# A hybrid decoder layer on one core: instruction order around the selection, paired memory scores, quarter-size merge tiles

## The chip, the core and the metric

The kernel runs on one core of a Trainium2 chip. Its engines work side by side, each through its own list of instructions in the order in which the program issued them: TensorE (PE, with its weight loads PEld), VectorE (DVE), ScalarE (ACT), GpSimd (POOL) and SyncE (SP), which starts the DMA transfers. They meet only at semaphores. The metric is the time of one execution in microseconds (us); lower is better.

## The reference, cut to what matters

```
h = x @ w_in                                  # 1024 x 1024 tokens, 14 column groups
# A: gated DeltaNet, 4 heads x 128, chunked delta rule
g    = -exp(a_log) * softplus(a + dt_bias);   g = cumsum(g) per chunk
m    = I + strict_lower(k_beta @ k^T * decay) # solved against v*beta and k_beta*exp(g)
S    = S * exp(g_last) + k_dec^T @ (u - w @ S)    # scan over the chunks
# B: sparse attention, 4 heads x 64 over a shared latent of rank 128
score = sum_j relu(q_idx_j . k_idx) * w_j     # indexer, 8 heads x 64, causal
idx   = top_k(score, 256)                     # which keys a query may see
o_s   = softmax(q_abs . c[idx] / 8 - slope * dist) @ c[idx], then @ w_uv
# C: cross attention, 4 heads x 64, into 256 memory tokens
o_m   = softmax(q_m @ k_m^T / 8) @ v_m
y = concat(rmsnorm(o_a) * silu, o_s * silu, o_m * silu) @ w_out
x = layernorm(alpha * x + y)
```

Instead of gathering, the kernel finds for every query the value of its 256th largest score and turns the scores into masks.

## The kernel before

The 1024 tokens are 8 blocks of 128. `make_plan` (L127) writes one list of steps such as `("proj", h, part, t, s)`; each engine walks the list and issues what it has to do for a step. So the order of a step in the list is its order in every engine's queue, and the list is all that sets the order. The stages, with their time in the profile:

- 0 to 80 us: loads, splitting of x and weights into a high and a low half (`split` on ScalarE, `low` on VectorE; three matmuls, L1025 to L1027, make one product), the projections for the indexer.
- 80 to 152 us: the index scores (`idx`): 2 matmuls into a bank (L1017), a ReLU on ScalarE (L1851), a weighted sum on VectorE (L1466). Between them stand projections of head 0, the memory keys and values (`kmT`, `vm`) and the gates (`gate_sums`: two matmuls, four small operations on VectorE L1546 to L1550, three exponentials on ScalarE L1881 to L1883; `knorm`).
- 152 to 575 us: for each of the 4 DeltaNet heads the inverse of a triangular matrix is merged in levels 4, 5 and 6. `M` multiplies (L1188), ScalarE copies the product out, `XY` multiplies with the copy (L1201, L1203), VectorE subtracts (L1630, L1632). Then comes a scan over 8 blocks (`scanV`, `scanS`). A scan step goes from PE to VectorE and back twice. The function `woven` (L228) puts projections of the next head (`proj`, `side`) between these steps as fill.
- In the same stretch the selection runs: 32 rounds, one for each bit of a float. A round counts, on ScalarE, the scores above a candidate for 6 blocks (L1863, in three groups of two blocks: `count`), then VectorE makes the next candidate (`update`, L1472 to L1489; in the last round a chain of dependent operations up to L1506). ScalarE of a round waits for VectorE's update, and the update waits for all six counts. `woven` puts a group of counts into a fill whenever `owed`, raised by `SELECT_RATE` per fill, reaches 1.
- After round 31: `reach` (one pass over the scores of a block, L1512), `threshold`, and six passes for each of 6 blocks (`dm`, L1668 to L1683), all on VectorE, woven into head 3.
- 575 to 821 us: attention by blocks in the order 3, 4, 2, 5, 1, 6, 0, 7: scores `sc`, memory scores `msc` (L1270; in two halves by head parity, 64 rows of contraction each), transposes, the latent sum `lat`, the output `o`, and the output projection `y` (L1340 to L1342) with layer norm. `merged` interleaves the queues of one block's attention, the next block's scores and the block before's projection. The weights of `y` are split in 8 pieces (`split out0` to `out7`: 128x1024 on ScalarE, then on GpSimd L2115).

PSUM has 8 banks, dealt out in turn by pools (`pools`): "D": 4 to 7 for `idx`, `At`, `M`, `XY`, `nw`, the scan and two of the three `tok` transposes; "A": 4, 5, 6 for `msc`, `mixT`, `pT`, `mpT`. A matmul into a bank waits until the use before it has been read.

## Time and profile before

| | us |
|---|---|
| median of 3 runs (817.15 to 823.08) | 821.11 |
| profiled execution, its own time | 822.64 |
| its span, first to last instruction | 820.8 |
| PE busy | 757.1 |
| VectorE busy | 493.4 |
| ScalarE busy | 454.9 |

The span is 1.84 us shorter than the time of the same execution. PE is the busiest engine by far, so the time is PE's own work, plus the time in which PE waits, plus what PE loses where its granted clock is 1.2 GHz instead of 2.4 GHz (0.50 in the column PEclk).

### The profile page before, as it was taken

The numbers are of one execution on the slowest core, as the hardware profiler recorded it, in microseconds if no ns is written. First come the engines' busy times: TensorE is split into PE (matmuls) and PEld (weight loads), VectorE is DVE, ScalarE is ACT, GpSimd is POOL, SyncE is SP. The second block draws the span as 40 slices with busy tenths as digits, with TensorE's granted clock in tenths as the row PEclk, the third lists the DMA queues.
The fourth block names the chain that finished last, engine by engine and source line by source line (L and its number), as shares of the span: only waits on it lengthen the run. The fifth ranks groups of instructions, "written<-read, shape, count | busy, mean of one in ns | idle before, by whom it ended". The sixth has DMA issues, their size and how long they took to land.

```text
span 820.8 us, 11387 instructions
## 1 busy us (share of the span) xinstructions
PE 757.1 (92%) x3940; PEld 623.1 (76%) x3940; DVE 493.4 (60%) x1076; ACT 454.9 (55%) x1027; POOL 178.6 (22%) x272
## 2 busy tenths in 40 slices
PE   6999999899899999988999898987789999989993
PEld 5888888688798788877798687865567777767772
DVE  5633889775557484564646449594744644754533
ACT  4532776787768975988568971222752332433310
POOL 0000000162003610251103520000376134312320
PEclk9999999999899999999899996999989999999997
DMA  9312111034002330024000351010951322231110
GB/s 362 117 52 78 51 39 65 0 98 119 26 27 68 85 116 26 27 81 135 26 27 27 93 161 40 26 46 25 334 161 40 110 71 86 77 94 52 65 51 26
DMA packets 63913, 65.86 MB, mean 80 GB/s; under 512 B 16368, under 2 KB 49392, under 8 KB 63472
## 3 DMA queue, kind: packets, MB, share of 16 engines
q1 hardware_dynamic: 63856, 65.13, 24.7%
q8 instruction: 32, 0.52, 0.3%
q14 instruction: 25, 0.20, 0.1%
HBM read 48.35 MB, written 16.78 MB: 79 GB/s over the span
## 4 chain that ended last, share of the span: by engine, by line
PE 60%; DVE 17%; ACT 11%; issue 10%; DMA 1%; POOL 0%; SPq 0%; ACTq 0%; DVEq 0%; POOLq 0%
PE bank L1025 8%; PE bank L1026 8%; PE bank L1027 8%; PE bank L1017 6%; ACT cst L1863 5%; PE bank L1340 4%; PE bank L1031 4%; PE bank L1341 4%; PE bank L1342 4%; PE bank L1290 3%; PE bank L1203 3%; DVE score L1466 2%; PE bank L1201 2%; PE bank L1188 2%; ACT ring_split L1780 1%
## 5 line engine op out<-in xcount | busy, mean ns | idle before, releaser
L1025 PE MATMUL bank<-x_hi,ring_split 128*128 128x512 f32 x480 | 201.4, 420 | 8.5 <-DVE x_lo L1415 7.3
L1026 PE MATMUL bank<-x_lo,ring_split 128*128 128x512 f32 x480 | 191.7, 399 | 0.0
L1027 PE MATMUL bank<-x_hi,ring_split 128*128 128x512 f32 x480 | 191.7, 399 | 0.0
L1863 ACT ACTIVATE cst<-score,sel 128x896 bf16<-128x896 f32 (+3 forms) x192 | 167.1, 874 | 34.2 <-DVE sel L1488 32.6
L1025 PEld LDWEIGHTS bank<-x_hi,ring_split 128*128 128x128 f32 x480 | 93.4, 195 | 25.2 <-DVE ring_split L1419 7.3
L1027 PEld LDWEIGHTS bank<-x_hi,ring_split 128*128 128x128 f32 x480 | 92.8, 193 | 20.7
L1026 PEld LDWEIGHTS bank<-x_lo,ring_split 128*128 128x128 f32 x480 | 93.5, 195 | 15.8
L1780 ACT ACTIVATE arena<-bank 128x512 f32<-128x512 f32 x77 | 44.0, 590 | 72.7 <-PE bank L1031 50.3
L2046 POOL TENSOR_TENSOR arena<-arena,hsc 128x512 f32<-128x512 f32 x8 | 8.3, 1038 | 269.7 <-ACT arena L1933 269.7
L1340 PE MATMUL bank<-w_out_hi,mix_hi 128*128 128x512 f32 x128 | 58.5, 457 | 5.4 <-DVE mix_lo L1729 5.4
L2033 POOL TENSOR_TENSOR arena<-arena,cst 128x512 f32<-128x512 f32 x24 | 32.6, 1377 | 103.2 <-PE bank L1188 53.3
L1466 DVE SCALAR_TENSOR_TENSOR score<-arena,wis,score 128x384 f32<-128x384 f32 (+3 forms) x70 | 46.0, 657 | 9.6 <-ACT arena L1851 3.2
L1341 PE MATMUL bank<-w_out_lo,mix_hi 128*128 128x512 f32 x128 | 51.2, 400 | 0.0
L1342 PE MATMUL bank<-w_out_hi,mix_lo 128*128 128x512 f32 x128 | 51.0, 398 | 0.0
L1031 PEld LDWEIGHTS bank<-cst,arena 128*128 128x128 f32 x320 | 38.7, 145 | 12.4 <-issue 6.8
L1031 PE MATMUL bank<-cst,arena 128*128 128x128 f32 x320 | 47.0, 281 | 1.0 <-ACT arena L1980 0.6
L1419 DVE TENSOR_TENSOR ring_split<-ring,ring_split 128x1024 fp32r<-128x1024 f32 x30 | 37.9, 1264 | 7.5 <-ACT ring_split L1780 7.1
L1851 ACT ACTIVATE arena<-bank 128x384 f32<-128x384 f32 (+3 forms) x80 | 36.6, 529 | 8.8 <-PE bank L1017 6.7
L1971 ACT ACTIVATE arena<-arena,misc 128x512 f32<-128x512 f32 (+7 forms) x32 | 24.8, 774 | 26.7 <-DVE misc L1698 26.6
L1472 DVE TENSOR_TENSOR sel<-sel 128x6 f32<-128x6 f32 x32 | 11.8, 368 | 42.3 <-ACT cst L1863 42.3
L1290 PE MATMUL bank<-arena,small 128*128 128x512 f32 x72 | 36.8, 602 | 0.3 <-DVE arena L1706 0.3
L1863 ACT ACTIVATION_READ_ACCUMULATOR cst<-score,sel 128x1 f32 x192 | 36.7, 191 | 0.0
(274 smaller groups left out, 1477.9 us busy)
## 6 DMA issues: line engine op xcount, KB each, us to landing
ring<-in_w_groups SPq DMA_DIRECT2D x30, 512.0 KB, 3.5
x_raw<-in_x_t SPq DMA_DIRECT2D x8, 512.0 KB, 8.8
side_z<-stage SPq DMA_DIRECT2D x16, 256.0 KB, 2.1
w_out_sb<-in_wout_t SPq DMA_DIRECT2D x2, 2048.0 KB, 11.1
zgT<-side_z SPq DMA_DIRECT2D x8, 512.0 KB, 3.9
qkvT<-in_x SPq DMA_DIRECT2D x8, 512.0 KB, 3.3
out_y<-arena SPq DMA_DIRECT2D x8, 512.0 KB, 2.9
ring<-in_wmem_t SPq DMA_DIRECT2D x2, 1024.0 KB, 4.6
```

The source lines that it names most:

```text
L1017: last = nc.tensor.matmul(dst, w, r, start=(i == 0), stop=(i == len(pairs) - 1))
L1025: nc.tensor.matmul(dst, hi, xh, start=(c == 0), stop=False)
L1026: nc.tensor.matmul(dst, hi, xl, start=False, stop=False)
L1027: last = nc.tensor.matmul(dst, lo, xh, start=False, stop=(c == KT - 1))
L1031: return nc.tensor.transpose(dst, src, ident[0:n, 0:n])
L1290: last = nc.tensor.matmul(ps(key)[:, :], sm[:, kt, 0:P], pTb[(order[e] - 1) % 3], start=(kt == 0), stop=(kt == b))
L1340: nc.tensor.matmul(ps(key)[:, :], mh, wout_hi[:, c, half], start=(c == 0), stop=False)
L1341: nc.tensor.matmul(ps(key)[:, :], mh, wout_lo[:, c, half], start=False, stop=False)
L1342: last = nc.tensor.matmul(ps(key)[:, :], ml, wout_hi[:, c, half], start=False, stop=(c == KT - 1))
L1466: last = v.scalar_tensor_tensor(score[:, at + lo:at + hi], r[:, 0:hi - lo], w, score[:, at + lo:at + hi], ALU.mult, ALU.add)
L1780: return sc.activation(dst, src, ACT.Copy, scale=scale)
L1863: sc.activation(signs[order[e] % 2][:, 0:w], score[:, score_at(b):score_at(b + 1)], ACT.Sign, scale=-1.0, bias=candidate[:, b - 2:b - 1], ...
```

## The change

- `gate_sums` stands some units earlier in the index stage; its three exponentials are a step of their own, `gate_exps`, that follows all index tiles.
- `SELECT_RATE` is 0.90 (0.88). In the fill before `M` of level 4 no counts are put; they come behind it (a fill of length 0).
- `reach` and `dm` are single steps, put in by a budget (`MASK_KEYS` keys per unit of fill) instead of pairs per fill.
- The last merge level multiplies 64x64 quarters: `M` and `XY` of level 6 use 64 rows and 64 columns of each block, and the copy is 64x256 (128x512).
- `msc` of both halves of a block is one step that alternates the two row halves; it waits for both banks first, and at block 3 only for the memory keys; the values are waited for at `o`.
- The splits of the output weights: two while block 3's attention runs (four), six in the next block.

```diff
-SELECT_RATE = 0.88
+SELECT_RATE = 0.90
+MASK_KEYS = 1350
@@ make_plan
-    selection += [[("reach", 7), ("reach", 2)], [("reach", 6), ("reach", 3)], [("reach", 5), ("reach", 4), ("threshold",)]]
-    selection += [[("dm", b, i), ("dm", b, i + 1)] for b in SELECT_ORDER for i in (0, 2, 4)]
+    selection += [[("reach", b)] for b in range(NB - 1, 2, -1)] + [[("reach", 2), ("threshold",)]]
+    selection += [[("dm", b, i)] for b in SELECT_ORDER for i in range(6)]
...
-    first_work = [*keys, [("kmT",)], [("gates",)], *queries, [("vm",)], [("silu", 0, 0)], [("gate_sums",)], [("knorm", 0)]]
+    first_work = [*keys, [("kmT",)], [("gates",)], *queries, [("gate_sums",)], [("vm",)], [("silu", 0, 0)], []]
...
+    add(("gate_exps",))
+    add(("knorm", 0))
...
+    def mask_cost(e):
+        return (e[1] + 1) * P * (2 if e[0] == "dm" and e[2] == 2 else 1)
+
+    def masks(keys):
+        owed[1] = min(owed[1] + keys, 2 * SEQ)
+        while selection and not due and owed[1] >= mask_cost(selection[0][0]):
+            owed[1] -= mask_cost(selection[0][0])
+            select()
...
-            if silus[0] == 0 and s[2]:
+            if selection and selection[0][0][0] != "count":
+                if s[2]:
+                    masks(int(MASK_KEYS * s[1]))
+            elif silus[0] == 0 and s[2]:
                 owed[0] -= select(int(owed[0] >= 1))
...
-        steps = [*pair("At", h), *pair("tok", h, 0), ("diag_load", h), 1, 1, *pair("tok", h, 2), 1, 1]
+        steps = [*pair("At", h), *pair("tok", h, 0), ("diag_load", h)]
+        steps += [1, 1, *pair("tok", h, 2), 1] if more else [("fill", 1, None)] * 2 + [*pair("tok", h, 2), ("fill", 1, None)]
+        steps += [("fill", 1, 0)]
...
-            steps += [*pair("M", h, s), 1.5, QUIET if s == NLEV - 1 and more else 1.5]
+            steps += [*pair("M", h, s), *([("fill", 0, SELECT_RATE)] if s == LEV0 else []), 1.5, QUIET if s == NLEV - 1 and more else 1.5]
...
-            at[place:place] = [[("msc", nb, 0)], [("msc", nb, 1)]]
+            at[place:place] = [[("msc", nb, 0), ("msc", nb, 1)]]
...
-            out = [[("split", f"out{i}")] for i in range(4)]
+            out = [[("split", f"out{i}")] for i in range(2)]
...
-                for i in range(4):
-                    out[i].append(("split", f"out{i + 4}"))
+                for i, at_unit in enumerate((0, 0, 1, 2, 4, 5)):
+                    out[at_unit].append(("split", f"out{i + 2}"))
@@ TensorE, M and XY of the last level
+                            last = nc.tensor.matmul(ps(e)[0:64, i * 64:(i + 1) * 64], uo[0:64, 64:P], x_[0:64, 0:64], start=True, stop=True)
...
+                            m1 = row(a, R_M1)[64:P, i * 64:(i + 1) * 64]
+                            last = nc.tensor.matmul(ps(e)[0:64, i * 64:(i + 1) * 64], m1, blk(row(a, R_Y), i)[64:P, 64:P], start=True, stop=True)
@@ TensorE, msc
-                            pe.wait_ge(side_mem_back, 32)
+                        pe.wait_ge(mem_keys_back, 16)
...
+                    for m in range(2):
+                        for i, half in enumerate(halves):
+                            rows_ = slice(64 * i, 64 * i + 64)
+                            last = nc.tensor.matmul(ps(half)[:, m * 256:(m + 1) * 256], q_mem(PLACE[b])[rows_, m, :],
+                                                    kmT[rows_, m * 256:(m + 1) * 256], start=True, stop=True)
@@ ScalarE
+                    if s == NLEV - 1:
+                        copy(row(a, R_M1)[64:P, 0:256], ps(e)[0:64, 0:256]).then_inc(release_of(e), 1)
```

How it moves instructions, at three places. First ScalarE's queue in head 0, before level 4: the L1863 rows are counts (two per group), the `arena<-bank 128x512 x2` row is the copy of the two `M` tiles. Before:

```order
L1780 ACTIVATE hbuf<-bank 128x512
L1863 ACTIVATE cst,sel<-score,sel 128x1024
L1863 ACTIVATE cst,sel<-score,sel 128x384
L1863 ACTIVATE cst,sel<-score,sel 128x896
L1863 ACTIVATE cst,sel<-score,sel 128x512
L1780 ACTIVATE arena<-bank 128x512 x2
L1863 ACTIVATE cst,sel<-score,sel 128x768
L1863 ACTIVATE cst,sel<-score,sel 128x640
```

And in the change (its lines are 37 further down):

```order
L1817 ACTIVATE hbuf<-bank 128x512
L1900 ACTIVATE cst,sel<-score,sel 128x1024
L1900 ACTIVATE cst,sel<-score,sel 128x384
L1817 ACTIVATE arena<-bank 128x512 x2
L1900 ACTIVATE cst,sel<-score,sel 128x896
L1900 ACTIVATE cst,sel<-score,sel 128x512
```

One group of counts stands behind the copies instead of ahead of them. The second place is VectorE's queue at the start of head 3. The row `arena<-bank,arena 128x512 x2` is the evacuation of the two `At` tiles; the rows on `sel` are the update of round 31. Before:

```order
L1399 TENSOR_TENSOR o_head<-o_head,bank 128x128 x2
L1373 TENSOR_TENSOR arena<-bank,arena 128x512 x2
L1472 TENSOR_TENSOR sel<-sel 128x6
L1483 TENSOR_TENSOR sel<-sel 128x6
L1484 TENSOR_SCALAR sel<-sel 128x6
```

And in the change, from the long custom operation of that update on:

```order
L1535 ISA sel<-sel 128x12
L1536 TENSOR_TENSOR sel<-sel 128x6
L1537 TENSOR_TENSOR sel<-sel 128x6
L1538 TENSOR_TENSOR sel<-sel 128x6
L1539 TENSOR_TENSOR sel<-sel 128x6
L1540 TENSOR_TENSOR sel<-sel 128x6
L1546 TENSOR_SCALAR qkvT,sel<-score,sel 128x1024
L1407 TENSOR_TENSOR arena<-bank,arena 128x512 x2
```

The whole update and the first `reach` now stand ahead of the two evacuations. The third place is PE's queue at the first memory scores (block 3), with the banks. Before:

```order
L1270 MATMUL bank4<-kmT_64,arena 128x256 x2
L1017 MATMUL bank2<-key_stack,q_hi_odd_blocks_67 128x320
L1017 MATMUL bank2<-key_stack,q_odd_blocks_lo_59 128x320
L1017 MATMUL bank3<-key_stack,q_hi_odd_blocks_67 128x320
L1017 MATMUL bank3<-key_stack,q_odd_blocks_lo_59 128x320
L1270 MATMUL bank5<-kmT_64,arena 128x256 x2
```

And in the change:

```order
L1302 MATMUL bank4<-kmT_64,arena 128x256
L1302 MATMUL bank5<-kmT_64,arena 128x256
L1302 MATMUL bank4<-kmT_64,arena 128x256
L1302 MATMUL bank5<-kmT_64,arena 128x256
L1039 MATMUL bank2<-key_stack,q_hi_odd_blocks_67 128x320
```

The two halves stand together and alternate between banks and row halves.

## Rows read from the trace of the kernel before

**Rows 1.** The page, part 1: busy us, share of the span, instructions.
```profile
PE 757.1 (92%) x3940; PEld 623.1 (76%) x3940; DVE 493.4 (60%) x1076; ACT 454.9 (55%) x1027; POOL 178.6 (22%) x272
```
**Rows 2.** Timeline of PE: start, us, what, [idle before <- releaser]; its waits.
```profile
148.63 0.79 PE L1017 MATMUL bank<-khi,q 128*128 128x512 f32 x1 [2.71 <-ACT arena L1851]
...
208.82 0.43 PE L1201 MATMUL bank<-arena 128*128 128x64 f32 x2 [2.47 <-ACT arena L1780]
...
398.71 0.43 PE L1201 MATMUL bank<-arena 128*128 128x64 f32 x2 [1.63 <-ACT arena L1780]
...
496.33 0.41 PE L1201 MATMUL bank<-arena 128*128 128x64 f32 x2 [1.91 <-DVE arena L1612]
...
544.52 0.80 PE L1238 MATMUL bank<-vnew,arena 128*128 128x128 f32 x2 [2.27 <-DVE vnew L1637]
...
558.25 0.79 PE L1238 MATMUL bank<-vnew,arena 128*128 128x128 f32 x2 [2.86 <-DVE vnew L1637]
...
582.17 1.13 PE L1270 MATMUL bank<-kmT,arena 64*128 64x256 f32 x4 [1.21 <-DMA vm<-side_mem]
...
601.43 1.08 PE L1309 MATMUL bank<-wuv,arena 128*128 128x64 f32 x8 [3.17 <-ACT arena L1780]
```
**Rows 3.** Stretches: span, busy us of PE, PEld, DVE, ACT, POOL, PEclk, DMA.
```profile
148.60:151.60 3.00, 2.97 (x8) 2.29 (x9) 2.68 (x4) 2.82 (x8) 0.00 (x0) 0.50 0.00 0
209.70:216.60 6.90, 6.90 (x31) 6.51 (x31) 5.31 (x15) 6.28 (x15) 0.00 (x0) 0.51 0.00 0
...
401.30:407.60 6.30, 6.30 (x22) 5.43 (x22) 5.87 (x15) 3.78 (x7) 0.00 (x0) 0.50 0.00 0
```
**Rows 4.** Timeline of VectorE: the last index sums.
```profile
148.61 5.88 DVE L1466 SCALAR_TENSOR_TENSOR score<-arena,wis,score 128x512 f32<-128x512 f32 x7 [1.02 <-ACT arena L1851]
```
**Rows 5.** Timeline of ScalarE: counts and the copies of M, heads 0 and 2.
```profile
206.46 1.03 ACT L1863 ACTIVATE cst<-score,sel 128x896 bf16<-128x896 f32 x1
...
208.19 1.06 ACT L1780 ACTIVATE arena<-bank 128x512 f32<-128x512 f32 x2
...
396.33 1.15 ACT L1863 ACTIVATE cst<-score,sel 128x1024 bf16<-128x1024 f32 x1 [4.14 <-DVE sel L1488]
```
**Rows 6.** Stretches around head 3, and the scan of head 2.
```profile
478.70:486.90 8.20, 7.81 (x49) 6.64 (x48) 1.77 (x5) 8.15 (x19) 0.00 (x0) 1.00 0.65 168
...
487.90:562.10 74.20, 66.01 (x329) 55.14 (x327) 63.07 (x112) 16.25 (x31) 4.42 (x4) 0.86 0.13 44
...
454.00:473.00 19.00, 14.76 (x84) 12.25 (x83) 10.18 (x34) 17.92 (x45) 8.90 (x31) 1.00 0.30 81
```
**Rows 7.** Timeline of VectorE: evacuation of At, update of round 31, reach, the masks' hole.
```profile
480.94 1.28 DVE L1373 TENSOR_TENSOR arena<-bank,arena 128x512 f32<-128x512 f32 x2
486.88 0.17 DVE L1472 TENSOR_TENSOR sel<-sel 128x6 f32<-128x6 f32 x1 [4.66 <-ACT cst L1863]
...
492.33 1.28 DVE L1512 TENSOR_SCALAR_CACHE_REDUCE qkvT<-score,sel 128x1024 f32<-128x1024 f32 x1
...
532.02 1.39 DVE L1560 SCALAR_TENSOR_TENSOR key_stack<-bank,key_stack 64x512 fp32r<-64x512 f32 x2 [4.64 <-ACT key_stack L1780]
```
**Rows 8.** Timeline of ScalarE: the last weight split ahead of block 3's output.
```profile
599.75 1.05 ACT L1780 ACTIVATE w_out_hi<-w_out_sb 128x1024 fp32r<-128x1024 f32 x1
```
**Rows 9.** Timeline of PE: M and XY of level 6 (head 0), one half of msc.
```profile
232.93 1.95 PE L1188 MATMUL bank<-arena 128*128 128x128 f32 x16
...
238.82 1.90 PE L1203 MATMUL bank<-arena 128*128 128x64 f32 x16
...
650.36 1.13 PE L1270 MATMUL bank<-kmT,qmT 64*128 64x256 f32 x4
651.41 0.33 PE L1031 MATMUL bank<-cst,arena 128*128 128x128 f32 x1
```
**Rows 10.** Waits over the whole span: who for whom, us in total, times, longest.
```profile
DVE sel L1472 <- ACT cst L1863: 42.3, 22, 4.7
...
ACT cst L1863 <- DVE sel L1488: 32.6, 22, 4.1
```

More of the change, by code:

```diff
@@ L237, in woven @@
             at += s[1]
-            owed[0] += s[2]
-            update()
+            owed[0] += s[2] or 0
+            if s[2] is not None:
+                update()
             while todo and n_units - len(todo) < n_units * at / whole:
@@ L1187, in _ @@
                     for i in range(4):
-                        last = nc.tensor.matmul(ps(e)[:, i * P:(i + 1) * P], blk(row(a, R_UO[s % 2]), i), blk(row(a, R_X), i), start=True, stop=True)
+                        uo, x_ = blk(row(a, R_UO[s % 2]), i), blk(row(a, R_X), i)
+                        if s < NLEV - 1:
+                            last = nc.tensor.matmul(ps(e)[:, i * P:(i + 1) * P], uo, x_, start=True, stop=True)
+                        else:
+                            last = nc.tensor.matmul(ps(e)[0:64, i * 64:(i + 1) * 64], uo[0:64, 64:P], x_[0:64, 0:64], start=True, stop=True)
                     last.then_inc(fill_of(e), 1)
@@ L1941, in _ @@
                     act.wait_ge(*filled(e))
[L1942 removed]
+                    if s == NLEV - 1:
+                        copy(row(a, R_M1)[64:P, 0:256], ps(e)[0:64, 0:256]).then_inc(release_of(e), 1)
+                    else:
+                        copy(row(a, R_M1), ps(e)[:, :]).then_inc(release_of(e), 1)
                 elif k == "nw":
```

53 lines of the change are left out of this document (28 added, 25 removed).

## The prediction, made before the changed kernel ran

> **What bounds the kernel now.** I read the page's first part first: PE is busy 757.1 of 820.8 us, VectorE 493.4, ScalarE 454.9 [rows 1]. PE is idle 63.9 in all, and that is where an edit of order can gain. Then PE's timeline with its waits: the long ones stand at four kinds of place, behind the last index tile, at the first multiply of a merge level (L1201), in head 3's scan (L1238) and at the entry to block 3's attention [rows 2]. Then the granted clock by stretches: behind such waits PE runs at 1.2 GHz for some us, for instance 6.9 us long behind the wait of 2.47 [rows 2, 3]. PE is busy there without a break and does half as much, so a stretch of 6.9 costs 3.4 beside the wait itself. Last, VectorE's and ScalarE's timelines at these places, for what the wait ends on [rows 4, 5, 7, 8]. The selection has its own pair of waits, VectorE for ScalarE 42.3 us and ScalarE for VectorE 32.6 [rows 10]; PE works through nearly all of them.
>
> **Part by part.** The sum goes against the profiled execution: span 820.8, own time 822.64. The median is 821.11, 1.5 less, and gains are taken off the median for the predicted time.
>
> *1. Gate exponentials behind the index tiles.* ScalarE held the ReLU for gate work that waited for VectorE; PE waited 2.71 for it and ran at half clock from 148.6 to 151.6, 1.5 lost [rows 2, 3]. Both together, 4.2, are the most that it can give. But VectorE is late itself there: its only idle in the last index sums is the 1.02 ahead of seven sums of 5.88 [rows 4], and what PE needs next is built on VectorE behind them. So the wait moves to head 0's first product instead of going. I take the 1.02 that VectorE can win: **-1.0**; ends 0 and -4.2.
>
> *2. One group of counts less ahead of the copies of M.* In head 0 PE waits 2.47 for the copies, which stand behind counts of about 1 us each; in head 2 1.63 [rows 2, 5]. Two counts behind the copies instead of ahead of them is 2 x 1.03: the first wait falls to about 0.6 (-1.8; a few tenths of the copies' 1.06 stay on the path), the second goes (-1.6). The half clock behind them costs 6.9/2 = 3.4 and 6.3/2 = 3.1 [rows 3]. Together -9.9. The counts don't vanish: they land later, in scans where ScalarE is busy 17.92 of 19.0 us [rows 6] and PE already has 4.2 idle. A quarter comes back there: **-7.4**; ends 0 and -9.9.
>
> *3. Head 3 and the masks.* From 487.9 to 562.1 PE is busy 66.0 of 74.2 at a mean clock of 0.86 [rows 6]; 0.14 x 74.2 = 10.4 of it is lost to the clock, so the work in it is 55.6 and 18.6 is the most that can go. Its waits for VectorE are 1.91, 2.27 and 2.86 [rows 2], each behind a pair of mask passes. VectorE is busy 63.1 of these 74.2, and only 1.77 of the 8.2 before [rows 6], so masks that start up to 6.4 earlier have room, and so has the hole of 4.64 at 532 [rows 7]. Against it stands a **new wait**: the update of round 31 (486.88 to 492.33, 5.45) and the first reach (1.28) now stand on VectorE ahead of the evacuation of At, which was done at 482.2 [rows 7]. Behind that evacuation are tok's second part on PE, which needs At's bank, and everything that follows it. PE has about 3 of the 7.81 us of work of that stretch in front of it, so it stalls about 6.7 - 3.0 = 3.7, and a half-clock stretch like the others' costs 3.4 more. That leaves 18.6 - 7.1 = 11.5. VectorE's chain (63.1 of busy time that cannot start before 481.5) ends no earlier than 544.6 even without one gap, and a scan step goes over it twice, so I take half: **-6.0**. Ends +3 (the stall of 7.1 and a gain of only 4 of the three waits' 7.0) and -12.
>
> *4. Memory values waited for later.* The wait of 1.21 for vm's transfer [rows 2] moves to block 3's output, 20 us on, where the transfer has landed: **-1.2**; end 0, if the keys are as late.
>
> *5. Fewer weight splits at the entry.* PE waits 3.17 at L1309 for a copy that stands behind a split of 1.05 [rows 2, 8]. Two of four splits are gone there. One was directly in front, so half of the wait or so goes: **-1.5**; ends 0 and -6.6, the wait and a half-clock stretch of 3.4 behind it.
>
> *6. Memory scores of both halves together.* One half costs PE 1.05 (650.36 to 651.41, where the next matmul starts) [rows 9]; 16 of them are 16.8. Each uses 64 of the 128 rows. If the two halves run side by side, 8.4 go; if PE takes them one after the other as now, nothing. No row of before shows two row halves in alternation, so these are the ends, 0 and -8.4. I take three quarters, **-6.4**: there are 8 passages with a start and a tail that only one half has, and the alternation is the arrangement in which two halves could overlap. The pair needs both banks at once: a few short waits at mixT go and one at the second bank comes, **-0.7**.
>
> On this the page "TensorEngine Tiling (Array Packing)" of the Trainium skill, section Key Properties, says that different tiles can load weights and multiply in parallel. By that rule term 6 would be the full 8.4, and the time 2 us less; no row of before shows it.
>
> *7. Quarter tiles of the last level.* M with 128 columns takes 1.95 for 16 records and XY with 64 columns 1.90 [rows 9]. Half the columns save 0.05. So columns are not what is paid for here, and fewer rows are not either as far as any row tells: **0**. Ends: if both halved, 4 heads x 3.85 / 2 = -7.7; if each change of tile shape costs about one record of 0.12, 16 changes are +1.9. The copy of M is half as wide on ScalarE and may give some tenths at L1203.
>
> The same page, section Instruction Overhead, gives each matmul a floor of about 60 cycles, and says not to take a tiling factor from a dimension that is already small. That speaks against this part, and the rows agree with it: 1.90 against 1.95. Key Properties adds that a change of tiling mode drains TensorE, which would be the +1.9 end.
>
> *8. Six splits in the next block.* GpSimd takes their low halves and each column half of y is multiplied as its split lands. If every one is in time, that costs nothing (the cover is block 4's attention), as four of them already do now. **0**; a late one costs a wait of about 1, the time of a split [rows 8].
>
> Sum: -1.0 - 7.4 - 6.0 - 1.2 - 1.5 - 6.4 - 0.7 = **-24.2**; 821.1 - 24.2 = 796.9, so **797**.
>
> **Rivals.**
>
> *A. The start of head 3 eats term 3* (0.16). The update and the reach hold At's banks longer than I think, because the counts of round 31 end no earlier than now: evacuation at 492.3 + 1.3, ten us late. The gain of 6.0 goes: 803. For it: [rows 7] shows VectorE waiting 4.66 for the last counts. Against: the rate of the selection is raised a little.
>
> *B. Row halves don't run side by side* (0.12). 6.4 come back: 803.3. For it: the 64-row halves now cost as much for each record as any other shape, so nothing shows that PE gives a free half away.
>
> *C. They overlap fully and short waits go too* (0.06): 2.0 less, 795. This is the skill's rule above.
>
> *D. The waits only move* (0.10). The M copies' 7.4 return in ScalarE's full scans, and head 3 and the exponentials give nothing, -1.2 - 1.5 - 6.4 - 0.7 = -9.8, and half of the overlap is gone too, -6.6: 814.5, within 1%. With the whole overlap it would be 811, just outside it.
>
> *E. Slower: the selection's rounds* (0.06). Each round is a closed loop, counts on ScalarE, update on VectorE [rows 10]. With copies ahead of counts, a round's last count comes later by up to the copies' 1.06 [rows 5]; if every one of 31 rounds grows by 1.1 us and the end of the selection pushes the masks and so head 3, that is +34 against -24: 831, 10 slower. It decides from 24.2/31 = 0.8 us a round. Against it: a fill before level 4 comes four times, not 31, and the 42.3 us of waiting in the loop can take up most of that.
>
> The forecast itself has 0.50, with a range of its own of 787 to 806.
>
> **Numbers.** The predicted time is the forecast's, 797. The unknown ends are 8.4 and 7.7 below for terms 6 and 7, 4 to 6 for terms 1, 3 and 5; they don't fall together, so the low end is 12 below: **785**. Upward, A and B together are 809, and part of D belongs to the range: **812**. Left out are E, the upper half of D, and the two tails: about 0.2. One per cent, about what a measurement of this kernel can tell from no change, is 8.2 us. Faster by more than that (below 812.9): forecast, A, B and C, 0.84. Within: D, 0.10. Slower: E, 0.06.
>
> **What would show it.** Term 1: the wait of 2.71 at L1017 is gone, and a similar one stands at head 0's first product. Term 2: the waits at L1201 of heads 0 and 2 under 1 us, and no stretch at 0.50 behind them. Term 3: a new PE wait of 3 to 4 us some us after 480, released by VectorE's evacuation of At (L1407); the waits of vnew below 1 us; the stage from 478.7 to 562.1 six us shorter. Term 4: no wait on vm. Term 5: L1309's counterpart under 2 us. Term 6: msc's two halves together take about 1.2 instead of 2.1. Term 7: 16 records of 64x64 at 1.9 to 2.0. I'm wrong if the new wait at head 3's start is over 8 us, if the pair of halves takes 2.1, or if quarter records cost about half, which would put the time near 789.

## The result, and the profile after

| | median, us | runs | against before (95% interval) |
|---|---|---|---|
| before | 820.67 | 817.15 to 823.08 | |
| changed | 793.17 | 790.73 to 794.88 | 0.9666 (0.9622 to 0.971) |

The change saves 27.5 us, or 3.3%. The prediction was 797 with a range of 785 to 812. The profiled execution took 792.68 us, its span is 790.9 (before: 820.8), so 29.9 us are to be explained.

The first part of the page of the changed kernel, against [rows 1]:

```profile
PE 729.5 (92%) x3940; PEld 597.4 (76%) x3940; DVE 484.8 (61%) x1076; ACT 454.6 (57%) x1027; POOL 181.7 (23%) x272
```

PE is busy 27.6 us less with as many instructions; its idle time fell by 2.3 only, from 63.7 to 61.4. So nearly all of the gain is PE working faster: at 2.4 GHz where it had 1.2, two row halves at once, smaller tiles. The clock is the largest part of it. The mean granted clock is 0.965 in the profile before and 0.987 in this one, which is 57 us at 1.2 GHz before and 21 after; half of the difference, 18 us, is my estimate of what the clock gave back. Most of the waits that I had counted off came back elsewhere.

The same by stage. I cut both traces where PE starts the product At of each head (L1175 before, L1197 after) and the first memory scores. Columns: span, busy us (and count) of PE, PEld, VectorE, ScalarE, GpSimd, granted clock, DMA share, GB/s. Before:

```profile
163.90:258.30 94.40, 91.19 (x503) 79.23 (x504) 58.26 (x132) 72.77 (x151) 23.07 (x43) 0.96 0.21 64
258.30:348.60 90.30, 88.53 (x532) 76.75 (x531) 55.83 (x132) 73.34 (x169) 24.12 (x43) 1.00 0.22 67
348.60:448.20 99.60, 93.46 (x532) 80.68 (x531) 56.45 (x135) 74.42 (x170) 23.68 (x43) 0.95 0.20 61
448.20:582.17 133.97, 116.56 (x613) 96.34 (x611) 89.00 (x197) 60.33 (x144) 20.63 (x43) 0.92 0.25 74
582.17:820.80 238.63, 215.68 (x1072) 163.44 (x1072) 125.50 (x293) 81.95 (x205) 81.94 (x91) 0.96 0.28 92
```

And after:

```profile
163.40:252.80 89.40, 87.22 (x503) 74.50 (x504) 57.65 (x132) 72.35 (x151) 23.55 (x43) 1.00 0.22 68
252.80:341.70 88.90, 87.27 (x532) 75.19 (x531) 55.99 (x139) 74.95 (x172) 24.30 (x43) 1.00 0.23 68
341.70:431.10 89.40, 87.11 (x532) 75.32 (x531) 53.52 (x135) 76.91 (x176) 24.49 (x43) 1.00 0.22 68
431.10:550.39 119.29, 107.89 (x614) 88.22 (x612) 84.95 (x189) 54.68 (x130) 22.19 (x43) 0.99 0.26 79
550.39:790.90 240.51, 208.84 (x1072) 158.47 (x1072) 124.45 (x293) 83.02 (x209) 81.97 (x91) 0.97 0.28 93
```

Up to the first cut 0.5 is gained; heads 0 to 3 gain 5.0, 1.4, 10.2 and 14.7. The last stage, attention, is **1.9 longer**, though its memory scores became 8.4 cheaper. That is the surprise of this result: 10 us were given back in a stage that the prediction had at -8.6 in all.

Where attention gave it back shows in PE's lines with the idle time before them (columns: count, busy us, mean ns, idle before and its releasers). Before, the output `o` and the output projection `y`:

```profile
L1309 PE MATMUL bank<-wuv,arena 128*128 128x64 f32 x64 | 8.1, 269 | 3.2 <-ACT arena L1780 3.2
L1340 PE MATMUL bank<-w_out_hi,mix_hi 128*128 128x512 f32 x128 | 58.5, 457 | 5.4 <-DVE mix_lo L1729 5.4
```

After:

```profile
L1342 PE MATMUL bank<-wuv,arena 128*128 128x64 f32 x64 | 9.0, 288 | 6.2 <-ACT arena L1817 6.2
L1374 PE MATMUL bank<-w_out_hi,mix_hi 128*128 128x512 f32 x128 | 57.3, 448 | 10.2 <-DVE mix_lo L1766 7.7 <-POOL w_out_lo L2155 1.9 <-issue 0.6
```

The idle time ahead of `o` grew by 3.0, ahead of `y` by 4.8.

PE's timeline after, at the places of [rows 2] and [rows 9]; in brackets the idle before and its releaser:

```profile
163.39 0.46 PE L1197 MATMUL bank<-arena,qkvT 128*128 128x128 f32 x2 [1.73 <-ACT arena L1817]
...
206.60 0.43 PE L1231 MATMUL bank<-arena 128*128 128x64 f32 x2 [0.74 <-ACT arena L1817]
...
228.55 1.14 PE L1214 MATMUL bank<-arena 64*64 64x64 f32 x16
229.62 0.50 PE L1047 MATMUL bank<-x_hi,ring_split 128*128 128x512 f32 x1
...
466.43 0.41 PE L1053 MATMUL bank<-cst,qkvT 128*128 128x128 f32 x2 [1.81 <-DVE arena L1407]
...
518.43 0.49 PE L1268 MATMUL bank<-vnew,arena 128*128 128x128 f32 x2 [1.50 <-DVE vnew L1674]
...
550.39 1.13 PE L1302 MATMUL bank<-kmT,arena 64*128 64x256 f32 x8
551.45 0.42 PE L1039 MATMUL bank<-key_stack,q_hi_odd_blocks 128*128 128x320 f32 x1
...
569.60 0.56 PE L1342 MATMUL bank<-wuv,arena 128*128 128x64 f32 x2 [4.96 <-ACT arena L1817]
...
596.58 0.50 PE L1374 MATMUL bank<-w_out_hi,mix_hi 128*128 128x512 f32 x1 [1.92 <-POOL w_out_lo L2155]
```

The wait for the copies of M is 0.74 instead of 2.47. Sixteen quarter records take 1.07 (228.55 to 229.62); the same records of [rows 9] take 1.71 from 232.93 to the next matmul at 234.64. Both halves of the memory scores together take 1.06. And there are waits that were not there, or were shorter: 1.81 at the start of head 3, 4.96 at block 3's output (3.17 before), 1.83 for `mix_lo` at 584.47, 1.92 for GpSimd.

### The profile page after: what moved, and what is told of

Its sections match the earlier page's. It is cut to its first block, busy times and chain, and to the rows that moved or that the text cites. A ratio compares the mean times of both kernels' runs of the same rounds, so it can differ in the third digit from the quotient of the medians.

```text
span 790.9 us, 11388 instructions
## 1 busy us (share of the span) xinstructions
PE 729.5 (92%) x3940; PEld 597.4 (76%) x3940; DVE 484.8 (61%) x1076; ACT 454.6 (57%) x1027; POOL 181.7 (23%) x272
## 4 chain that ended last, share of the span: by engine, by line
PE 62%; DVE 14%; ACT 11%; issue 9%; POOL 2%; DMA 1%; SPq 0%; DVEq 0%; ACTq 0%; POOLq 0%
PE bank L1047 10%; PE bank L1049 10%; PE bank L1048 10%; PE bank L1039 5%; ACT cst L1900 4%; PE bank L1053 4%; PE bank L1374 3%; DVE score L1500 3%; PE bank L1375 3%; PE bank L1376 3%; PE bank L1323 2%; PE bank L1233 2%; PE bank L1231 2%; PE bank L1212 2%; POOL w_out_lo L2155 2%
## 5 line engine op out<-in xcount | busy, mean ns | idle before, releaser
L1047 PE MATMUL bank<-x_hi,ring_split 128*128 128x512 f32 x480 | 198.1, 413 | 8.2 <-DVE x_lo L1449 7.3
L1049 PE MATMUL bank<-x_hi,ring_split 128*128 128x512 f32 x480 | 189.4, 395 | 0.0
L1048 PE MATMUL bank<-x_lo,ring_split 128*128 128x512 f32 x480 | 189.1, 394 | 0.0
L1047 PEld LDWEIGHTS bank<-x_hi,ring_split 128*128 128x128 f32 x480 | 91.5, 191 | 24.6 <-DVE ring_split L1453 7.3
L1049 PEld LDWEIGHTS bank<-x_hi,ring_split 128*128 128x128 f32 x480 | 91.2, 190 | 20.1
L1048 PEld LDWEIGHTS bank<-x_lo,ring_split 128*128 128x128 f32 x480 | 91.7, 191 | 15.3
L1817 ACT ACTIVATE arena<-bank 128x512 f32<-128x512 f32 (+1 forms) x77 | 42.1, 565 | 65.4 <-PE bank L1053 53.6
L1374 PE MATMUL bank<-w_out_hi,mix_hi 128*128 128x512 f32 x128 | 57.3, 448 | 10.2 <-DVE mix_lo L1766 7.7
L1053 PE MATMUL bank<-cst,arena 128*128 128x128 f32 x320 | 45.4, 278 | 3.5 <-DVE arena L1633 2.0
L1374 PEld LDWEIGHTS bank<-w_out_hi,mix_hi 128*128 128x128 f32 x128 | 24.2, 189 | 21.9 <-DVE mix_lo L1766 9.8
```

Source lines behind the costliest of these rows:

```text
L1047: nc.tensor.matmul(dst, hi, xh, start=(c == 0), stop=False)
L1048: nc.tensor.matmul(dst, hi, xl, start=False, stop=False)
L1049: last = nc.tensor.matmul(dst, lo, xh, start=False, stop=(c == KT - 1))
L1053: return nc.tensor.transpose(dst, src, ident[0:n, 0:n])
L1374: nc.tensor.matmul(ps(key)[:, :], mh, wout_hi[:, c, half], start=(c == 0), stop=False)
L1817: return sc.activation(dst, src, ACT.Copy, scale=scale)
```

## The experiments

Twelve kernels ran, in three groups (1 to 4, 5 to 8, 9 to 12), each group on one chip beside the kernel before, whose median there was 818.78, 820.29 and 820.70. Each time stands beside its ratio to that, with its 95% interval; kernels 8 and 12 were executed only once and have none. Most kernels are the changed one with one part undone; the changed kernel's ratio is 0.9666. Where PE's clock makes the spans noisy I read the stage, not the whole.

**1. Memory scores: does the alternation matter?**

```diff
-                    for m in range(2):
-                        for i, half in enumerate(halves):
+                    for i, half in enumerate(halves):
+                        for m in range(2):
```

> The changed kernel with one difference: the four matmuls of a pair of memory scores stand half after half (0,0,1,1), no longer in alternation (0,1,0,1). Same banks, waits and place. In the changed kernel a pair takes PE about 1.1 us where each half took 1.05. Theory A (two row halves overlap only when neighbours in the queue use different rows): in turn, the pair costs about 2.1 (only one border between unlike rows), 8 pairs x 1.0 = 8 us longer, near 801. Theory B (it is enough that both stand together, PE runs ahead whatever the order): a pair stays at 1.1 to 1.3, near 793 to 795.

Measured: 790.79 us, 0.9669 (0.9637 to 0.97); span 790.6. PE's timeline of it:

```profile
560.72 1.14 PE L1302 MATMUL bank<-kmT,qmT 64*128 64x256 f32 x8
561.79 1.13 PE L1323 MATMUL bank<-arena,small 128*128 128x512 f32 x2
```

A pair takes 1.07 here too. Theory B holds: it is enough that the four matmuls stand together. The order inside the pair is worth nothing. Since this kernel times as the changed one does, it is also that kernel's stand-in on this chip.

**2. Quarter tiles undone.** `M`, `XY` and the copy of level 6 at full size:

```diff
-                        if s < NLEV - 1:
-                            last = nc.tensor.matmul(ps(e)[:, i * P:(i + 1) * P], uo, x_, start=True, stop=True)
-                        else:
-                            last = nc.tensor.matmul(ps(e)[0:64, i * 64:(i + 1) * 64], uo[0:64, 64:P], x_[0:64, 0:64], start=True, stop=True)
+                        last = nc.tensor.matmul(ps(e)[:, i * P:(i + 1) * P], uo, x_, start=True, stop=True)
...
-                        copy(row(a, R_M1)[64:P, 0:256], ps(e)[0:64, 0:256]).then_inc(release_of(e), 1)
...
```

> The changed kernel with M, XY and the copy of level 6 back at full size (128 rows, 128 or 64 columns). Theory A (the quarters are cheaper themselves): 16 records go back from 1.07 (start to next start) to 1.71 and 1.74, 8 x 0.65 = 5.2 us longer, and the wider copy may add a few tenths: near 798.5. Theory B (my term of 0; the gain elsewhere only makes it look so, drains of the tile change eat it): no more than 1 us, 793 to 794.

Measured: 796.26 us, 0.9732 (0.9701 to 0.9762), 5.5 over kernel 1 on the same chip. In the trace heads 0 to 2 (At of head 0 to At of head 3) take 270.7 instead of 267.7, a good 1.0 for each head; four heads make 4 of the 5.2 that the records would give. Theory A holds; the term that I had at 0 is worth 4 us by the stages and 5.5 by the medians.

**3. Four splits ahead of block 3's output again.**

```diff
-            out = [[("split", f"out{i}")] for i in range(2)]
+            out = [[("split", f"out{i}")] for i in range(4)]
...
-                for i, at_unit in enumerate((0, 0, 1, 2, 4, 5)):
-                    out[at_unit].append(("split", f"out{i + 2}"))
+                for i in range(4):
+                    out[i].append(("split", f"out{i + 4}"))
```

> The changed kernel with four weight splits back in block 3's attention and four, one by one, in the next. In the changed kernel PE waits 4.95 us at block 3's output (longer than the 3.17 of before) and 1.92 for GpSimd's last low half in block 4's stage, with half clock behind both. Theory A (fewer splits ahead of the copy help, the longer wait has another cause, the memory exponentials of both halves of block 4 ahead of it): the wait at block 3's output grows by 1 to 2, to 6 or 7, the wait on GpSimd goes with its half clock (1.9 + 1.9), sum 2 faster to 1 slower: 791 to 794. Theory B (splits are no part of it): the first wait stays 4.9 to 5.1, the second goes, 789.5.

Measured: 787.05 us, 0.9626 (0.9594 to 0.9659), 3.7 **under** kernel 1 and faster than either theory had it. Attention takes 235.9 instead of 240.5. The wait at `o` is 5.49, so more splits do lengthen it, but only by half a microsecond; the wait of 1.92 for GpSimd is gone, and so is one of 1.83 for `mix_lo`. This part of the change costs, it does not gain. VectorE's timeline of this kernel shows something else:

```profile
561.49 0.69 DVE L1739 TENSOR_REDUCE misc<-bank 128x2 f32<-128x512 f32 x1 [1.31 <-PE bank L1302]
562.22 0.86 DVE L1740 TENSOR_SCALAR misc<-misc 128x2 f32<-128x2 f32 x1
562.99 0.68 DVE L1739 TENSOR_REDUCE misc<-bank 128x2 f32<-128x512 f32 x1
563.71 1.67 DVE L1740 TENSOR_SCALAR misc<-misc 128x2 f32<-128x2 f32 x1
```

The operation on two columns takes 0.86 and 1.67, where it takes 0.17 elsewhere (kernel 9, below). GpSimd is making low halves at that time (four, from 560.70 to 569.97), and ScalarE's exponentials wait for these two operations.

**4. Counts as before.** Rate 0.88, no group of counts moved behind the copies of `M` (both at once, so the two are not separated):

```diff
-SELECT_RATE = 0.90
+SELECT_RATE = 0.88
...
-        steps += [("fill", 1, 0)]
+        steps += [1]
...
-            steps += [*pair("M", h, s), *([("fill", 0, SELECT_RATE)] if s == LEV0 else []), 1.5, QUIET if s == NLEV - 1 and more else 1.5]
+            steps += [*pair("M", h, s), 1.5, QUIET if s == NLEV - 1 and more else 1.5]
```

> The changed kernel with the counts as before: rate 0.88, no group of counts moved behind the copies of M of level 4. Theory A (my term 2): waits of 1.6 to 2.5 for the copies of M come back in two heads with half clock behind, and the gain of head 2's stage (10.2 us, of which 1.3 are the quarter tiles) goes: 7 to 10 us longer, 800 to 803. Theory B (the gain of head 2 is chance of order in the scan, waits for vnew): 2 to 5 us longer, 795 to 798. If the selection then ends inside head 3 later by its lower rate, the masks add 1 to 3 to either.

Measured: 803.73 us, 0.9835 (0.9799 to 0.9871), 12.9 over kernel 1; span 801.1, 10.2 over the changed kernel's. The waits are back, as in [rows 2]:

```profile
208.35 0.48 PE L1231 MATMUL bank<-arena 128*128 128x64 f32 x1 [2.46 <-ACT arena L1817]
...
376.20 0.38 PE L1272 MATMUL bank<-dn_s,arena 128*128 128x128 f32 x1 [2.35 <-DVE vnew L1674]
...
396.21 0.32 PE L1231 MATMUL bank<-arena 128*128 128x64 f32 x1 [1.63 <-ACT arena L1817]
```

Theory A holds, at its upper end; head 3 starts 10.3 later. Of that head 0 has 5.4 and head 2 has 4.4. In head 0 the wait has its half clock behind it (granted clock 0.50 from 208 to 218). In head 2 it has none (1.00 from 399 to 409, where the kernel before had 0.66): its 4.4 are the waits of 1.63 and of 2.35 for `vnew`, and the second I had not counted. The kernel says something of term 3 too. The update of round 31 begins at 483.9, 42.5 us into head 3, where it is 29.9 in the changed kernel and 38.7 before, and head 3 takes 119.2, as in the changed kernel (119.3).

**5. Mask passes in pairs again** (reach stays single, so that no mask is written while head 2's scan still reads that storage).

```diff
-    selection += [[("dm", b, i)] for b in SELECT_ORDER for i in range(6)]
+    selection += [[("dm", b, i), ("dm", b, i + 1)] for b in SELECT_ORDER for i in (0, 2, 4)]
...
-            if selection and selection[0][0][0] != "count":
+            if selection and selection[0][0][0] == "reach":
```

> The changed kernel with the mask passes (dm) in pairs again, one pair per fill without the budget by keys; reach stays single, and the start of head 3 stays as changed. Theory A (single passes by length are what took the waits for vnew from 2.3 and 2.9 down to 1.3 to 1.5 and the half clock behind them away): waits of 2 to 3 come back at L1268 in head 3's scan, with half clock behind at least one, 3 to 6 us longer: 796 to 799. Theory B (the earlier end of the selection is what helps, VectorE has room anyway): under 1.5 longer, 793 to 794.5.

Measured: 797.37 us, 0.9719 (0.9683 to 0.9755); span 796.2. PE's timeline in head 3's scan:

```profile
520.21 0.79 PE L1268 MATMUL bank<-vnew,arena 128*128 128x128 f32 x2 [3.10 <-DVE vnew L1674]
533.19 0.49 PE L1268 MATMUL bank<-vnew,arena 128*128 128x128 f32 x2 [1.27 <-DVE vnew L1674]
538.36 1.10 PE L1151 MATMUL bank<-arena,wuk 128*128 128x512 f32 x2 [2.85 <-ACT stage L1874]
```

Head 3 takes 123.7 (432.9 to 556.6), against 117.7 in kernels 6 and 7: 6.0 for the pairs alone, two waits of 3 instead of 1.5 and less, and 6 us of half clock behind the first. (The profile of the changed kernel has 119.3 there, with a stretch at half clock behind its wait of 1.81.) Theory A holds.

**6. Gate sums and exponentials together, last.**

```diff
-    first_work = [*keys, [("kmT",)], [("gates",)], *queries, [("gate_sums",)], [("vm",)], [("silu", 0, 0)], []]
+    first_work = [*keys, [("kmT",)], [("gates",)], *queries, [("vm",)], [("silu", 0, 0)], [("gate_sums",), ("gate_exps",)], [("knorm", 0)]]
...
-    add(("gate_exps",))
-    add(("knorm", 0))
```

> The changed kernel with gate sums and exponentials together again as one of the last steps of the index stage, and the keys' norm behind them. Theory A (my term 1: the wait moves to head 0's first products and only about 1 us is won): the wait of 2.7 at the last index tile comes back with half clock, the waits of 1.42, 0.57 and 1.72 at 156 to 163 go or shrink, 0 to 1.5 longer in sum, 793 to 794.7. Theory B (the moved exponentials win the wait and the clock): 3 to 4 longer, 796 to 797.

Measured: 791.89 us, 0.9658 (0.9615 to 0.9701); no difference. The old wait is back (2.70 at 148.94, released by ScalarE's ReLU), the new ones at 157 to 163 are gone or 0.6, and At of head 0 starts at 164.2 instead of 163.4 (163.0 in kernels 5 and 7, of the same group). Theory A: the part is worth 0.8 to 1.2 at its place, too little for the medians to show.

**7. Block 4's memory scores behind block 3's output**, on kernel 3.

```diff
-            at[place:place] = [[("msc", nb, 0), ("msc", nb, 1)]]
+            if n:
+                at[place:place] = [[("msc", nb, 0), ("msc", nb, 1)]]
...
         add(("o", b))
         if n == 0:
+            add(("msc", nb, 0))
+            add(("msc", nb, 1))
```

> The kernel with four weight splits in block 3's attention (787.05 us) and one more difference: block 4's pair of memory scores stands behind block 3's output instead of ahead of its last latent sums. Theory A (the wait of 5.5 us at block 3's output is the pair's work of both halves, two reductions on VectorE slowed by GpSimd and four exponentials on ScalarE, ahead of the latent copy): the wait falls to about 1, and the half clock of 7 us behind it goes, 4.5 + 3.5 = 8 us; block 4's first transposes wait 2 to 4 us for the exponentials instead: 4 to 6 faster, 781 to 783. Theory B (the wait has its cause in the last split or the bank): it stays at 4 or more, and the time is 787 or longer.

Measured: 792.59 us, 0.9658 (0.9616 to 0.97). Theory A was wrong: the wait at `o` falls only from 5.49 to 3.96, and a new one of 2.99 stands at block 4's first transposes (this one theory A had). VectorE's timeline again has the reason:

```profile
562.99 0.08 DVE L1732 DVE_READ_ACCUMULATOR2_ANT misc<- 128x1 f32 x1
563.11 2.29 DVE L1737 TENSOR_TENSOR misc<-misc 128x1 f32<-128x1 f32 x1
565.43 0.15 DVE L1738 TENSOR_SCALAR misc<-misc 128x1 f32<-128x1 f32 x1
```

With the reductions of `msc` out of the way, the next small operation between SBUF operands waits for GpSimd instead, 2.29 for one column; GpSimd's four low halves run from 563.03 to 572.29. So the pair's work is 1.5 of the wait, and most of the wait stands without it.

**8. What makes a quarter cheap: rows or columns?** `M` of level 6, in odd heads all 128 rows and 64 weight columns, in even heads 64 rows and all 128 weight columns.

```diff
-                            last = nc.tensor.matmul(ps(e)[0:64, i * 64:(i + 1) * 64], uo[0:64, 64:P], x_[0:64, 0:64], start=True, stop=True)
+                            if h % 2:
+                                last = nc.tensor.matmul(ps(e)[0:64, i * 64:(i + 1) * 64], uo[:, 64:P], x_[:, 0:64], start=True, stop=True)
+                            else:
+                                last = nc.tensor.matmul(ps(e)[:, i * 64:(i + 1) * 64], uo[0:64, :], x_[0:64, 0:64], start=True, stop=True)
...
```

> The changed kernel with M of level 6 cut in one direction only: in heads 0 and 2 64 of 128 rows of contraction, all 128 weight columns; in heads 1 and 3 64 weight columns, all 128 rows. 64 moving columns in all heads; XY stays a quarter. 16 records of M take 1.07 us from start to next start as quarters, 1.71 as 128x128. Theory A (fewer weight columns are what is cheaper, the load of weights is the step that is paid): heads 1 and 3 1.1, heads 0 and 2 1.7. Theory B (fewer rows: the two passes of a record can overlap, or the load goes by rows): heads 0 and 2 1.1, heads 1 and 3 1.7. Theory C (it takes both): 1.7 in all, or 1.4 in each.

Measured once, 792.77. PE's timeline of head 0 (the rows cut) and of head 1 (the weight columns cut), each with the instruction behind it:

```profile
228.13 2.00 PE L1217 MATMUL bank<-arena 64*128 64x64 f32 x16
230.05 0.50 PE L1047 MATMUL bank<-x_hi,ring_split 128*128 128x512 f32 x1
...
317.79 1.15 PE L1215 MATMUL bank<-arena 128*64 128x64 f32 x16
318.86 0.50 PE L1047 MATMUL bank<-x_hi,ring_split 128*128 128x512 f32 x1
```

64 rows: 1.92 for 16 records. 64 weight columns: 1.07, all that the quarter gives; heads 2 and 3 repeat both. The weight loads of the two (columns: count, busy us, mean ns, idle before):

```profile
L1217 PEld LDWEIGHTS bank<-arena 64*128 64x128 f32 x32 | 3.7, 188 | 0.3 <-issue 0.3
L1215 PEld LDWEIGHTS bank<-arena 128*64 128x64 f32 x32 | 2.0, 138 | 0.5 <-issue 0.5
```

A load at full size takes 192 ns and a quarter's 134, so the columns set it and the rows don't. Theory A holds. Why 64 rows take 1.92, 0.2 more than the 1.71 of full size, no run shows. The Trainium skill says on its page "TensorE: Matmul & The Clock Gate", section "Step-by-step: what each phase is for", that the time of a weight load scales with the column count and that the row count doesn't matter. The trace agrees, 138 ns against 188.

**9. The first four splits behind block 3's output**, the other four in the next block as in kernel 3.

```diff
-            out = [[("split", f"out{i}")] for i in range(2)]
+            out = []
...
-                for i, at_unit in enumerate((0, 0, 1, 2, 4, 5)):
-                    out[at_unit].append(("split", f"out{i + 2}"))
+                for i in range(4):
+                    out[i].append(("split", f"out{i + 4}"))
...
             add(("deltanet_scale", b))
+            for i in range(4):
+                add(("split", f"out{i}"))
```

> The changed kernel with the first four weight splits behind block 3's output (and its scale), the other four in the next block as in the kernel with four splits (787.05 us). Theory A (the wait of 5 us at that output is made of two things: a split directly ahead of the latent copy, 1.05, and small VectorE operations that take 0.9 to 2.3 instead of 0.17 while GpSimd makes the low halves): both go, the wait falls from 4.95 to 2 to 2.5, the VectorE operations at L1740 take 0.17, ScalarE makes the four splits in its idle time behind; 2 to 5 faster than with four splits ahead, 782 to 785, if GpSimd's 19 us of low halves are still in time; each late one costs 1 to 2. Theory B (the memory exponentials of both halves alone are the wait): it stays at 4 or more and the low halves come late, 790 or more.

Measured: 787.49 us, 0.96 (0.9559 to 0.9641). VectorE's timeline at the same place as in kernel 3:

```profile
563.32 0.69 DVE L1741 TENSOR_REDUCE misc<-bank 128x2 f32<-128x512 f32 x1 [1.31 <-PE bank L1304]
564.04 0.17 DVE L1742 TENSOR_SCALAR misc<-misc 128x2 f32<-128x2 f32 x1
564.12 0.68 DVE L1741 TENSOR_REDUCE misc<-bank 128x2 f32<-128x512 f32 x1
564.84 0.17 DVE L1742 TENSOR_SCALAR misc<-misc 128x2 f32<-128x2 f32 x1
```

The wait at `o` falls from 4.96 to 2.46 as theory A has it: 1.55 is the blocked VectorE operation, 1 the split in front; the rest is the four exponentials (1.9) and the copy (0.6) on ScalarE. GpSimd does nothing from 562.6 to 570.4. But the low halves now come late (waits of 0.91, 0.36 and 0.67), and attention takes 236.8, no better than kernel 3's 235.9. So the time misses theory A's 782 to 785.

**10. No mask pass ahead of head 3**, on kernel 3.

```diff
-                if s[2]:
+                if s[2] and rate == 1.0:
                     masks(int(MASK_KEYS * s[1]))
```

> The kernel with four splits in block 3's attention (787.05 us), with no mask pass ahead of head 3: the first reach (1.3 us) stands behind the evacuation of At, not ahead. Theory A (the wait of 1.8 at tok's second part is the update and this reach, and the half clock that some runs show behind it comes with it): the wait falls to about 0.5, 1.3 to 3 faster, 784 to 786. Theory B (the update alone does it, or the reach costs its 1.3 elsewhere, since VectorE has no room in head 3): wait 1.8 or the waits for vnew longer, no change, 786.5 to 788.

Measured: 786.97 us, 0.9594 (0.9559 to 0.9629). The wait at tok's second part is 0.50 instead of 1.8, and head 3 takes 116.4 (430.2 to 546.6) instead of 117.8: the 1.3 that theory A gives. Kernel 3's profile has no half clock there either. The median can't tell the two kernels apart; only the trace can.

**11. Both**: the edits of kernels 9 and 10 on the changed kernel.

```diff
-            out = [[("split", f"out{i}")] for i in range(2)]
+            out = []
...
-                if s[2]:
+                if s[2] and rate == 1.0:
```

> Both of these at once: splits behind block 3's output, first reach behind the evacuation of At. If the two places are independent, the gains add, 780 to 784; if one of them is nothing, the time is the other's.

Measured: 785.76 us, 0.9573 (0.9529 to 0.9618), the fastest of all medians, 1% under the changed kernel; its interval doesn't touch that one's. Head 3 takes 116.4 and the wait at `o` is 2.46, so both effects are there in the trace; the waits for low halves are 1.74, 0.37 and 0.68. The time can't be told from kernels 3, 9 and 10, and it is above the 780 to 784 at which the gains would add.

**12. Memory values waited for at the scores**, in the changed kernel.

```diff
                         pe.wait_ge(mem_keys_back, 16)
+                        pe.wait_ge(mem_values_back, 16)
```

> The changed kernel with the wait for the memory values back at block 3's memory scores. Theory A (term 4): the transfer lands at about 551.8 (issue at 547.38, 4.4 to landing) and PE is there at 550.4, so a wait of 1.2 to 1.5 on it comes back and the time is as much longer. Theory B (the wait only takes the place of a wait for VectorE some us on): the wait is there, but block 3's output is reached at the same time as before.

Measured once, 793.58. A wait of 1.32 on vm's transfer stands at 550.43; from there to `o` it takes 18.56 instead of 19.21. So the part is worth 1.3 at its place, of which half comes back before `o`: between the two theories.

## Why the prediction was right, and which terms were not

The time came out 4 under the forecast, well inside. Of the rivals, A's stall exists but is small, B is refuted, and C's overlap came, though not its short waits. D had the copies' gain come back in the scans, which kernel 4 refutes, but its title holds for attention. E's loss did not come. The terms behind it, in the order of the sum:

| term | predicted | measured | from |
|---|---|---|---|
| 1 gate exponentials | -1.0 | -0.8 to -1.2 | kernel 6 |
| 2 copies of M ahead of counts | -7.4 | -10.2 (spans), -12.9 (medians) | kernel 4 |
| 3 head 3 and masks | -6.0 | -12.4 (stage) | stages, kernel 5 |
| 4 memory values later | -1.2 | -1.3, net -0.7 | kernel 12 |
| 5 and 8 splits moved | -1.5 | +3.7 | kernel 3 |
| 6 paired memory scores | -6.4, -0.7 | -8.4, 0 | trace |
| 7 quarter tiles | 0 | -4 to -5.5 | kernel 2 |

- **Term 1** held to the letter: the wait moved, 1.43, 0.57 and 1.73 at 157 to 163.
- **Term 2**: in head 0 it went as told, wait and half clock. In head 2 kernel 4 brings the wait back without a half clock, and a wait of 2.35 for `vnew` that I had not counted is there instead, so that the size agrees there is partly luck. The discount was wrong: I took a quarter off for counts that land in full scans. They do land there (ScalarE is 2.5 busier in head 2), and PE waits less in them than before.
- **Term 3**: head 3's stage is 14.7 shorter; 1.0 of it are the quarters and 1.3 the memory values, which leaves 12.4, a little past the end of -12. Kernel 5 gives 6.0 of that to single mask passes. For the rest no kernel undoes the part alone. An earlier end of the selection can be little of it: kernel 4 ends the selection late again, and its head 3 is no longer than the changed kernel's. What the traces show is that the wait of 1.91 at 496.33 [rows 2] and 6.8 us lost to half clock behind it (granted clock 0.54 and 0.61 from 496 to 512) are gone in every kernel that has `reach` as single steps. The new wait that I named is there, at the predicted place, released by the predicted instruction, but 1.81 long, not 3.7. PE had about 2.8 us of work in front of it, close to the 3 that I gave it; what I had too long was the update: 3.30 (460.97 to 464.27), not 5.45. Of the 5.45 before, two operations that take 0.17 in the changed kernel took 1.26 and 1.22. The second of them, and GpSimd beside it:

```profile
490.40 1.22 DVE L1502 TENSOR_TENSOR sel<-sel 128x6 uint32<-128x6 uint32 x1
489.07 2.52 POOL L2033 TENSOR_TENSOR arena<-arena,cst 128x512 f32<-128x512 f32 x2 [11.39 <-PE bank L1188]
```

  So "half of 11.5" was too careful in its price of the stall, and half was a choice without a row.
- **Term 5** was the step that failed, with its sign: undone in kernel 3, it makes the kernel 3.7 faster. I had read the wait of 3.17 as the split directly ahead of the copy and took half of it off. VectorE's timeline of the kernel before said otherwise, had I looked:

```profile
594.18 2.30 DVE L1703 TENSOR_SCALAR misc<-misc 128x2 f32<-128x2 f32 x1
...
597.71 1.09 DVE L1703 TENSOR_SCALAR misc<-misc 128x2 f32<-128x2 f32 x1
```

  The copy stands behind exponentials, these behind a VectorE operation on two columns, and that one is held up while GpSimd makes the low halves (from 594.10 to 603.37 here; 0.17 free, 1.72 in the changed kernel). Fewer splits shift GpSimd's work, they don't take it away. Four exponentials stand ahead of the copy in both kernels. Before, two of them had run when PE went idle at 598.26; with both halves of the scores at once, all four run (566.09 to 568.02) while PE waits from 564.64 on. What did speak for caution was in the text as term 8, "a late one costs a wait of about 1": it cost 1.92 and a stretch of 6.5 us at a granted clock of 0.74.
- **Term 6**: full overlap, 8 pairs at 1.07. By busy time of the 64 records it is 18.1 to 9.7. The Trainium skill's rule on parallel tiles ("TensorEngine Tiling (Array Packing)", Key Properties), which I had as rival C, agrees with the trace, and my three quarters were a hedge. The short waits did not go: PE waits 2.3 ahead of the later pairs (1.16, twice), and 2.5 before.
- **Term 7**: [rows 9] shows that moving columns cost nothing, 1.90 against 1.95, and I extended this to "fewer rows and columns are nothing". But both of those rows load 128 weight columns; no row of before had 64, so the rows could not carry the 0. It should have had a size and a chance, as the end of -7.7 did. The Trainium skill's floor of 60 cycles (same page, Instruction Overhead) is about the moving side and does not contradict what was measured. Its drain on a change of tiling mode (Key Properties) no run separates: the 1.07 of 16 records, of the quarters as of kernel 8's 128 rows by 64 columns, holds whatever the change costs. The sign that I had named, "if quarter records cost about half", came near: 1.07 is 0.63 of 1.71.

The errors have both signs: terms 2, 3, 6 and 7 gave some 15 us more than predicted, and attention took 10 of that back. That the sum came out at 27.5 for 24.2 is in good part luck. Of the signs that I had listed, three failed: the waits for `vnew` stayed above 1 (1.50, 1.26, 1.29), the wait at block 3's output was to be under 2, and the quarters were to take 1.9 to 2.0.

Three numbers of the prediction are off by themselves: PE's idle time is 63.7, not 63.9; three quarters of 8.4 is 6.3, not 6.4; and of term 6's end of -8.4 only 2.0 lies below what the sum took, so that the low end of 785 rests on less than its sentence says.

**Still open.** Heads 0 to 2 take 284.3 in the kernel before and 278.0 in kernel 4. The quarter tiles are 3.0 of that difference. Nearly all of the rest is half clock that the one run has and the other hasn't, behind waits that both have: 1.7 behind the wait of 2.35 (377 to 381) and 3.4 behind the wait of 1.63 (399 to 409) are lost only before, and behind the wait of 2.46 in head 0 kernel 4 loses 1.6 more. Of the 10 us that attention gave back, kernel 3 returns 4.6. What is left there is idle time: PE is idle 28.8 us in kernel 3's attention and 23.0 before, 2.3 of the difference at block 3's `o`, the rest in waits of about 1 and less. Ahead of `y` the wait for `mix_lo` is 5.9 in kernel 3 (5.4 before, 7.7 in the changed kernel). No kernel keeps the halves of the memory scores apart with the rest changed, so what pairing them costs in waits is not separated.

## What to carry to other kernels

Read an operation of the waited-for engine at its duration, not at its place in the order: a two-column operation of 1.7 us where its twins take 0.17 names another culprit than the engine that PE is said to wait for. Before pricing a smaller matmul at nothing, see that some row varies the dimension that is cut; here it was the weight columns that paid. And a gain in one stage is worth reading off by stage, since the next one can give it back while the total looks as forecast.

## What the runs showed of the hardware

**GpSimd's long operations hold small ones of VectorE up.** In the changed kernel:

```profile
564.34 1.72 DVE L1740 TENSOR_SCALAR misc<-misc 128x2 f32<-128x2 f32 x1
...
582.01 2.32 DVE L1766 TENSOR_TENSOR mix_lo<-arena,mix_hi 128x512 fp32r<-128x512 f32 x1 [2.07 <-ACT mix_hi L1817]
```

and GpSimd at the same time as the first:

```profile
563.69 2.34 POOL L2155 TENSOR_TENSOR w_out_lo<-w_out_sb,w_out_hi 128x1024 fp32r<-128x1024 f32 x1 [0.82 <-ACT w_out_hi L1817]
```

The small operation ends at 566.06, with GpSimd's at 566.03. Operations of VectorE that read a PSUM bank beside it keep their time (0.69 for the reductions of `msc` in kernel 3), and so does an operation on a single column that reads one SBUF tile (0.15 at 584.84, in the middle of a record of GpSimd). The Trainium skill, page "SBUF — State Buffer", section "Who interferes with whom", has this as a port pair that the two share under an exclusive lock. The end times agree with that, and kernel 9, where no low half is made at that time, shows 0.17.

**The granted clock is not decided by the last wait.** Head 0 of the changed kernel and of kernel 7 is the same queue with the same waits (0.73 and 0.79 at 196, 0.74 and 0.73 at L1231 and its counterpart). From 209 to 215 the changed kernel:

```profile
209.00:215.00 6.00, 5.56 (x31) 4.47 (x30) 4.20 (x12) 5.38 (x11) 0.00 (x0) 1.00 0.00 0
```

kernel 7:

```profile
209.00:215.00 6.00, 6.00 (x20) 5.13 (x20) 4.61 (x13) 5.38 (x13) 0.00 (x0) 0.50 0.00 0
```

31 matmuls against 20 in the same 6 us. Kernel 5 has the stretch too. Kernels 1 to 3 and 8 to 12, with the same queues up to there, have not (granted clock 1.00 from 208 to 216), and kernel 1 even waited longer at 196 (1.09). The other way round, kernel 4 and the kernel before have the same wait of 1.63 in head 2, with a granted clock of 1.00 and 0.66 behind it. The changed kernel's own executions spread the same way: a span of 788.9 at a mean clock of 0.987, one of 793.1 at 0.979. So a stretch at 1.2 GHz behind a wait may be there or not, and one profile fixes a term that rests on it only to about 3 us; the 3.4 that I took off for it in term 2 was fair as a mean at best.
